# The first stage of a fused four-layer block: filler products at the start, small tables before tile 1, the turns of mem behind the third tile, index heads in two groups

## The reference

```python
h = x @ w_in                        # q_a, c_kv, q_idx, k_idx, w_idx, q_b, k_b, v_b, f_in
log_f = log_sigmoid(f_in + b_f);  cum_f = cumsum(log_f)
idx   = einsum('bthd,bsd->bths', q_idx, k_idx)          # 8 index heads of 64
score = einsum('bth,bths->bts', w_idx, relu(idx))       # causal, then top 64 keys
_, sel = top_k(score, 64)
# 8 heads of latent attention on the selected keys, with a bias by distance
# 8 heads of causal attention with cum_f[t] - cum_f[s] added to the logits
m = concat(o_a, o_b) @ w_o
mem_n = rmsnorm(mem, mem_norm_g)    # used from layer 2 on
```

## Time and profile before

| | us |
|---|---|
| median of three runs (1380.58 to 1381.6) | 1381.14 |
| the profiled execution | 1381.37 |
| its span, first to last instruction | 1380.1 |
| PE busy | 1346.4 |
| DVE busy | 1019.9 |
| ACT busy | 783.8 |
| POOL busy | 180.9 |

### The profile page before, as it was taken

The page is one execution under the profiler, slowest core; times in us unless marked ns, Lnnn a source line. Parts: engine busy times, 40 slices in busy tenths (PEclk is TensorE's granted clock), DMA queues, the critical chain, the costliest instruction groups (busy, mean ns, idle before and its releaser), DMA issues.

```text
span 1380.1 us, 20700 instructions
## 1 busy us (share of the span) xinstructions
PE 1346.4 (98%) x8171; PEld 1162.7 (84%) x8171; DVE 1019.9 (74%) x1684; ACT 783.8 (57%) x1260; POOL 180.9 (13%) x155
## 2 busy tenths in 40 slices
PE   7999999999999999999999999999999999899998
PEld 7886888888897888887977788888789998688887
DVE  5865588777887787777777577766567997777675
ACT  5654266555443666563667466555557785565553
POOL 4860300000200000000034200000302224000000
PEclk9999999999999999999999999999999999899999
DMA  8522255654563555553432165555344445355552
GB/s 317 222 85 116 99 206 213 231 195 175 195 234 123 213 214 214 185 197 136 185 123 93 44 231 213 214 184 194 141 171 165 147 143 194 123 189 199 188 195 76
DMA packets 37215, 240.85 MB, mean 175 GB/s; under 512 B 4096, under 2 KB 6528, under 8 KB 9728
## 3 DMA queue, kind: packets, MB, share of 16 engines
q1 hardware_dynamic: 37120, 239.54, 47.2%
HBM read 236.89 MB, written 2.64 MB: 174 GB/s over the span
## 4 chain that ended last, share of the span: by engine, by line
PE 88%; DVE 6%; ACT 2%; issue 2%; DMA 1%; POOL 1%; SPq 0%; DVEq 0%; ACTq 0%; POOLq 0%
PE ps L385 23%; PE ps L437 16%; PE ps L390 12%; PE ps L448 8%; PE ps L365 5%; PE ps L372 5%; PE ps L366 5%; PE ps L607 2%; PE ps L602 2%; PE ps L954 1%; DVE wlo L318 1%; PE ps L1865 1%; PE ps L580 1%; ACT whi L295 1%; PE ps L2173 1%
## 5 line engine op out<-in xcount | busy, mean ns | idle before, releaser
L318 DVE TENSOR_TENSOR wlo<-raw,whi 128x2048 fp32r<-128x2048 f32 (+1 forms) x178 | 398.7, 2246 | 106.6 <-ACT whi L295 104.5
L295 ACT ACTIVATE whi<-raw 128x2048 fp32r<-128x2048 f32 x203 | 385.8, 1904 | 83.0 <-PE ps L448 40.1
L385 PE MATMUL ps<-XS,whi 128*128 128x512 f32 x1408 | 338.4, 393 | 0.7 <-DVE XS L653 0.7
L385 PEld LDWEIGHTS ps<-XS,whi 128*128 128x128 f32 x1408 | 262.8, 189 | 54.6 <-issue 1.8
L437 PE MATMUL ps<-whi,MS 128*128 128x512 f32 x960 | 233.6, 391 | 0.0
L437 PEld LDWEIGHTS ps<-whi,MS 128*128 128x128 f32 x960 | 177.5, 188 | 35.9 <-issue 0.4
L303 POOL TENSOR_TENSOR wlo<-raw,whi 128x512 fp32r<-128x512 f32 x114 | 155.4, 1396 | 283.4 <-ACT whi L295 195.2
L390 PEld LDWEIGHTS ps<-XS,wlo 128*128 128x128 f32 x1408 | 180.5, 191 | 6.9
L390 PE MATMUL ps<-XS,wlo 128*128 128x256 f32 x1408 | 182.6, 283 | 0.0
L365 PE MATMUL ps<-XS,whi 128*128 128x256 f32 x672 | 166.9, 288 | 0.0
L366 PE MATMUL ps<-XS,whi 128*128 128x256 f32 x672 | 163.0, 283 | 0.0
(11 more groups left out here) (319 smaller groups left out, 1523.8 us busy)
## 6 DMA issues: line engine op xcount, KB each, us to landing
raw<-in_up SPq DMA_DIRECT2D x88, 1024.0 KB, 4.8
raw<-in_down SPq DMA_DIRECT2D x44, 1024.0 KB, 4.8
raw<-in_hg_t SPq DMA_DIRECT2D x16, 1024.0 KB, 4.8
raw<-in_od_t SPq DMA_DIRECT2D x8, 1024.0 KB, 5.2
raw<-in_ev_a SPq DMA_DIRECT2D x6, 1024.0 KB, 9.0
raw<-in_wa_o SPq DMA_DIRECT2D x6, 1024.0 KB, 4.9
raw<-in_hg_o SPq DMA_DIRECT2D x6, 1024.0 KB, 4.8
raw<-in_ev_o SPq DMA_DIRECT2D x4, 1024.0 KB, 5.8
```

What stands on the lines that cost most here:

```text
L295: ac.activation(parts_of(m)[0][:, 0:w], raw[m % NRAW][:, 0:w], ACT.Copy).then_inc(w_hi)
L318: ve.tensor_tensor(lo[:, c], r[:, c], hi[:, c].bitcast(F32), ALU.subtract).then_inc(w_lo_v)
L385: pe.matmul(banks[i][:, 0:512], hi[:, c], XS[:, k, 0:512], start=(k == 0), stop=False)
```

## The change

- Eight bf16 products of ones, 512 columns, stand ahead of the turns of x on PE. The ones are written by DVE into `gp`, which is unused then.
- One-hot table and `rel_bias` are loaded by one DMA each, in three copies, between tile 0 and tile 1 instead of behind it. The load of tile 3 is issued ahead of the mask and the large constants.
- On PE the turn of the gate rows (L1081) and tile 2 come ahead of `mem_pe`, and the index heads, formerly all between tiles 2 and 3, come as heads 0 to 3 behind tile 3 and 4 to 7 behind tile 4, each head by itself.
- On ACT the split of tile 4 and both copies of the index queries come ahead of `mem_act`, the split of tile 5 ahead of the heads; the log-sigmoid and the copies of tile 3 come between heads 3 and 4, the split of tile 6 behind head 7.
- On DVE the forget row comes between heads 3 and 4.

```diff
@@ -825,6 +825,7 @@
         rel, relp = ar[0:96, 9024:9032], ar[0:96, 9032:9036].bitcast(BF16)
         BIAS_BANK = [0, 1, 2, 3, 6, 7, 2, 3]
         r_pt = mark("r_pt")
+        idle = gp[:, 0:256].bitcast(BF16)
         x_bank = [[6, 7], [2, 3]]
 
         def bias_rows_pe(heads):
@@ -849,6 +850,9 @@
                 last.then_inc(m_tp.up())
 
         def prelude_pe():
+            pe.wait_ge(busy.sem, 1)
+            for _ in range(8):
+                pe.matmul(bank[0][:, :], idle[:, 0:128], idle, start=True, stop=True)
             pe.wait_ge(d_id, 16)
             for tt in range(2):
                 pe.wait_ge(d_x[tt], 16)
@@ prelude_dve
             ve.memset(mhalf, -0.5).then_inc(half.up())
+            ve.memset(idle, 1.0).then_inc(busy.up())
             for tt in range(2):
                 for q in range(2):
                     hi, lo, bv = x_views(tt, q)
@@ -903,7 +908,7 @@
         def prelude_pool():
             po.wait_ge(half.sem, 1)
 
-            po.wait_ge(d_oh, 96)
+            po.wait_ge(d_oh, 32)
             po.tensor_copy(relp, rel).then_inc(r_pt.up())
             po.wait_ge(r_pt.sem, 1)
             po.tensor_tensor(rel[32:64], rel[32:64], relp[32:64], ALU.subtract).then_inc(r_pt.up())
@@ -922,15 +927,17 @@
             sp.dma_start(cc[:, 0:128], T["c_f32"][:, 0:128]).then_inc(d_id, 16)
             for i in range(2):
                 sp.dma_start(xn[:, i, :], T["x"][0, 128 * i:128 * i + 128]).then_inc(d_x[i], 16)
+            sp_weights(0)
+            hot, par = T["c_onehot"], T["c_par"]
+            sp.dma_start(onehot, bass.AP(tensor=hot.tensor, offset=hot.offset, ap=[[0, 3], [384, 32], [1, 384]])).then_inc(d_oh, 16)
+            sp.dma_start(rel, bass.AP(tensor=par.tensor, offset=par.offset + PC["relb"][0],
+                                      ap=[[0, 3], [NPC, 32], [1, 8]])).then_inc(d_oh, 16)
             sp_weights(1)
             sp.dma_start(pc[:, :], T["c_par"]).then_inc(d_pc, 16)
-            a, b = PC["relb"]
-            for i in range(3):
-                sp.dma_start(onehot[32 * i:32 * i + 32], T["c_onehot"]).then_inc(d_oh, 16)
-                sp.dma_start(rel[32 * i:32 * i + 32], T["c_par"][0:32, a:b]).then_inc(d_oh, 16)
             sp_weights(2)
             for i in range(2):
                 sp.dma_start(gb[:, i, :], T["mem_2"][0, 128 * i:128 * i + 128]).then_inc(d_mem[i], 16)
+            sp_weights(3)
             sp.dma_start(mask, T["c_mask"]).then_inc(d_cb, 16)
             sp.dma_start(cc[:, 128:], T["c_f32"][:, 128:]).then_inc(d_cc, 16)
             sp_weights(4)
@@ -1072,31 +1079,18 @@
             bias_rows_pe(range(6))
             project(ea + 1, bank[5])
             bias_rows_pe((6, 7))
-            mem_pe()
             pe.wait_ge(b_out.sem, 6)
-            project(ea + 2, bank[6])
             pe.wait_ge(e_ac.sem, 1)
-            pe.wait_ge(x_lo.sem, 4)
             for tt in range(2):
                 ins = pe.transpose(bank[7][:, 16 * tt:16 * tt + 16], FW[0:16, 128 * tt:128 * tt + 128], ident[0:16, 0:16])
             ins.then_inc(e_fw.up())
-            for h in range(0, 8, 2):
-
-                pe.wait_ge(e_ac.sem, 3 + h // 4)
-                if h >= 4:
-                    pe.wait_ge(e_re.sem, h - 2)
-                else:
-                    pe.wait_ge(m_ev.sem, 8)
-                for tt in range(2):
-                    a, b = esegs[tt]
-                    c = 256 * (h // 2) + 128 * tt
-                    for r in range(2):
-                        q = slice(64 * r, 64 * r + 64)
-                        ins = pe.matmul(bank[(h + r) % 4][:, a:b], QI[q, c:c + 128], KI[q, 0:b - a], start=True, stop=True)
-                        if tt == 1:
-                            ins.then_inc(e_ix.up())
+            project(ea + 2, bank[6])
+            mem_pe()
+            pe.wait_ge(e_ac.sem, 2)
             project(ea + 3, bank[4])
+            index_heads(range(0, 4))
             project(ea + 4, bank[5])
+            index_heads(range(4, 8))
             project(ea + 5, bank[6])
             pe.wait_ge(e_wi.sem, 1)
             project(ea + 6, bank[7])
@@ -1140,6 +1134,22 @@
                     latent_query(i - 6)
             output(eo, 8, ms_ready(E0, lambda k: (k + 4) % 8))
 
+        def index_heads(heads):
+            for h in heads:
+                if h < 4:
+                    pe.wait_ge(e_ac.sem, 3)
+                    pe.wait_ge(m_ev.sem, 8)
+                else:
+                    pe.wait_ge(e_ac.sem, 4)
+                    pe.wait_ge(e_re.sem, h - 3)
+                r = h % 2
+                q = slice(64 * r, 64 * r + 64)
+                for tt in range(2):
+                    a, b = esegs[tt]
+                    c = 256 * (h // 2) + 128 * tt
+                    ins = pe.matmul(bank[h % 4][:, a:b], QI[q, c:c + 128], KI[q, 0:b - a], start=True, stop=True)
+                ins.then_inc(e_ix.up())
+
         def score_b(o, h):
             c = 256 * h
             pe.wait_ge(e_ac.sem, max(AT_QB[h // 2], AT_KB[h // 2]))
@@ -1210,6 +1220,13 @@
                 pe.matmul(ePAIR[p % 2][64 * r:64 * r + 64, 0:256], WV[:, 64 * (h + r):64 * (h + r) + 64], OA[r], start=True,
                           stop=True).then_inc(e_po.up())
 
+        def index_act(heads):
+            for h in heads:
+                ac.wait_ge(e_ix.sem, h + 1)
+                if h >= 2:
+                    ac.wait_ge(e_sc.sem, 2 * h - 2)
+                ac.activation(RR[h % 2], bank[h % 4][:, 0:384], ACT.Relu).then_inc(e_re.up())
+
         def even_act():
             def out_of(m, i, dst, scale=1.0):
                 ac.wait_ge(w_done, DONE[m])
@@ even_act: weights and QI
-                if j:
-                    mem_act()
                 ac.wait_ge(w_done, DONE[ea + 1 + j])
                 ac.activation(QI[:, 512 * j:512 * j + 512], bank[5 + j][:, :], ACT.Copy, scale=0.125).then_inc(e_ac.up())
-            for h in range(8):
-                ac.wait_ge(e_ix.sem, h + 1)
-                if h >= 2:
-                    ac.wait_ge(e_sc.sem, 2 * h - 2)
-                ac.activation(RR[h % 2], bank[h % 4][:, 0:384], ACT.Relu).then_inc(e_re.up())
+            mem_act()
             act_weights(ea + 5)
+            index_act(range(0, 4))
             z = slice(0, 104)
             ac.wait_ge(e_fz.sem, 1)
             ac.wait_ge(e_fw.sem, 1)
@@ -1256,6 +1268,7 @@
             out_of(ea + 3, 0, CT)
             ac.wait_ge(d_skw, 16)
             heads_of(ea + 3, 1, QX, 0, 0.125)
+            index_act(range(4, 8))
             for j in range(3):
                 act_weights(ea + 6 + j)
                 heads_of(ea + 4 + j, 0, KX, j)
@@ -1299,14 +1312,8 @@
 
         e_sc = mark("e_sc")
 
-        def even_dve():
-            ve.wait_ge(m_tp.sem, 4)
-            for r in range(2):
-                ve.memset(hx4(KX, r)[64 - 64 * r:128 - 64 * r], 0.0).then_inc(dv.up())
-            ve.wait_ge(e_fw.sem, 1)
-            ve.tensor_scalar(WI, bank[7][:, 0:32], float(np.float32(8 ** -0.5)), None, ALU.mult).then_inc(e_wi.up())
-            ve.wait_ge(e_wi.sem, 1)
-            for h in range(8):
+        def index_dve(heads):
+            for h in heads:
                 r = RR[h % 2]
                 ve.wait_ge(e_re.sem, h + 1)
                 for tt in range(2):
@@ -1317,6 +1324,27 @@
                     else:
                         ve.wait_ge(e_sc.sem, e_sc.n - 1)
                         ve.scalar_tensor_tensor(S[:, a:b], r[:, a:b], w, S[:, a:b], ALU.mult, ALU.add).then_inc(e_sc.up())
+
+        def even_dve():
+            ve.wait_ge(m_tp.sem, 4)
+            for r in range(2):
+                ve.memset(hx4(KX, r)[64 - 64 * r:128 - 64 * r], 0.0).then_inc(dv.up())
+            ve.wait_ge(e_fw.sem, 1)
+            ve.tensor_scalar(WI, bank[7][:, 0:32], float(np.float32(8 ** -0.5)), None, ALU.mult).then_inc(e_wi.up())
+            ve.wait_ge(e_wi.sem, 1)
+            index_dve(range(0, 4))
+            z = slice(0, 104)
+            ve.wait_ge(e_ac.sem, 1)
+            ve.tensor_scalar(FZ[z, :], FW[z, :], col("bf", 0, 104), None, ALU.add).then_inc(e_fz.up())
+            ve.wait_ge(e_ab.sem, 1)
+            ve.tensor_scalar(FZ[z, :], FZ[z, :], 0.0, None, ALU.min).then_inc(dv.up())
+            ve.wait_ge(dv.sem, dv.n)
+            ve.wait_ge(e_ln.sem, 1)
+            ve.tensor_tensor(FZ[z, :], FZ[z, :], FW[z, :], ALU.subtract).then_inc(dv.up())
+            ve.wait_ge(dv.sem, dv.n)
+            ve.wait_ge(d_cc, 16)
+            ve.tensor_tensor_scan(FW[z, :], C("ones", 104), FZ[z, :], 0.0, ALU.mult, ALU.add).then_inc(dv.up())
+            index_dve(range(4, 8))
             ve.wait_ge(d_cc, 16)
             ve.wait_ge(e_sc.sem, e_sc.n)
             ve.tensor_tensor(S[:, 0:128], S[:, 0:128], C("cmf"), ALU.add).then_inc(dv.up())
@@ even_dve, ahead of the memsets of QX: the forget row, L1336 to L1345, is gone from here
...
```

12 lines of the change are left out of this document (1 added, 11 removed).

## The result

The changed kernel takes 1398.73 us, the median of six runs from 1394.3 to 1403.6, beside 1381.37 for the kernel before on the same chip (six runs, 1376.7 to 1383.9): 1.0127 times as long, with an interval of [1.0109, 1.0145], 17.4 us more. I had forecast 1378.2 and a range to 1381.8; the time is far outside it and on the other side. The profiled execution took 1394.3 us (span 1393.0), the shortest of the six, 12.9 us above the one of before; what the profile explains is therefore these 12.9 us and not all of the 17.4. Two executions of the record, one of e11 at 4712.6 us and one of the kernel before at 1904.6, were in a slow state, far from all others, and count in no ratio.

What follows compares the result with a forecast made beforehand. PE, 98% busy, was taken as the bound, with savings only in its first 90 us: 3.0 + 0.5 + 1.0 + 2.7 = 7.2 us, cut by late DVE to 2.9; 1381.14 - 2.9 = 1378.2 us, range 1375.2 to 1381.8.

Steps and rivals of the forecast that it cites:

- turns of mem: PE's mem turns moved behind the third tile: 3.33 us become two bias rows and 16 unwaited turns, 1.0 us gained.
- a first relu after 40: Stated sign of a wrong forecast: head 0's relu on ACT before 37 or after 40; 38.5 was expected.
- POOL against DVE: DVE's L1363 beside POOL's run: left at its old 2.71 us, or waiting until POOL idles at 83.6, same sum.
- Four heads: ... 4.0 us: DVE's first four index heads, begun at 39.1, take 4.0 us, to 43.1.
- slower rival: Tile 5's load shares its queue with tile 6's and the store, landing about 41.4: 1384.0 us, chance 0.10.
- Products of ones: Filler on PE before x lands, to raise the clock: tile 0 ends 3.0 us earlier, bounds 0 and 3.5.
- Small tables: Six DMAs become two ahead of tile 1, delaying it 0.4 us; PE's wait for POOL's casts goes, 0.5 us.
- Heads in two groups: PE's index heads between tiles: cost 3.2 us instead of 5.96, 2.7 less; bounds of new cost 3.2 and 6.4.
- ACT splits tile 5 ahead of head 0: ACT splits tile 5 from 36.5 to 38.4 before head 0, so DVE begins the heads 2.9 us late.
- Tile 5 and 6 chain, POOL idle between them: Late split of tile 6 (50.6 to 52.5) makes POOL, with nothing between tiles 5 and 6, begin tile 6 at 52.6.
- One constant from 90 us on: From 90 us on, the profiles before and after should differ by one constant, a gain of 2.9 us.
- PE at tile 6: PE could take tile 6 at 50.3, waits 2.2 and 1.9 us for its parts, ends it at 60.2 instead of 63.5.

Runs made afterwards that it cites:

- e11: Changed kernel with POOL holding tile 3 until mem is scaled and tile 12 until the mask is written, tile 5's load before the bias table's store: 1380.7 us.
- e1: Changed kernel with POOL starting tile 3's low part only when DVE has scaled mem's rows: 1390.1 us, ratio 1.0068.
- e2: Changed kernel with tile 3's load back behind the mask and constants: 1393.4 us, ratio 1.0090.
- e7: Kernel before with only tile 3's load moved ahead of the mask and constants: 1386.5 us, ratio 1.0050.
- e4: Changed kernel without products of ones, with old table loads and tile 3's load at its old place; only the new engine orders stay: 1390.2 us, ratio 1.0068.
- e8: Changed kernel with only tile 5's load issued ahead of the bias table's store: 1392.1 us, ratio 1.0083.
- e10: e1 with a second POOL wait, tile 12's low part starting only when DVE has written the mask: 1384.8 us, ratio 1.0032.
- e16: e11 with a third POOL wait, tile 5's low part starting only when the first four heads are done: 1378.7 us, ratio 0.9988.
- e5: Kernel before with only the eight products of ones and their memset added: 1380.0 us, ratio 0.9993.
- e17: e10 with ACT's split of tile 5 moved behind the first four heads: 1380.0 us, ratio 0.9994.
- e15: e11 with a third POOL wait, tile 5's low part starting only behind DVE's first update of head 4: 1385.6 us, ratio 1.0041.
- e6: Kernel before with only both small tables loaded by two DMAs ahead of tile 1: 1383.1 us, ratio 1.0010.
- e9: e1 with tile 5's load issued ahead of the bias table's store: 1387.1 us, ratio 1.0043.

## Why the prediction was wrong

The step that failed is the sentence on the turns of mem: "DVE's root of the squares ... is done by 27.3, some 0.6 earlier than before". I kept the root's length (3.9 us, 21.64 to 25.52), though the same change loads tile 3 sooner and so puts POOL beside it. It was done at 36.1, and mem was scaled at 37.5. e1, e2 and e7 show this from both sides. The number itself was misread: before, the root was done at 25.52 and mem scaled at 26.98, and the 27.9 that I took off from is the end of the bias copies behind them. The test that I had named, a first relu after 40, came true at 50.81.

Next, "POOL against DVE". I had seen that L1363 took 2.71 us and left it there "at the old length", or waiting for a POOL run that ends at 83.6, "the sum is the same". Both halves failed: the run no longer ends with tile 11, because a late DVE lets tile 12 join it, and shut out to the end costs 7.65 us (e1, e2, e4, e8). In the profiled execution of the changed kernel the threshold itself got in at 1.48, and the mask group lost only 1.9. By e10 against e1 the term is worth 5 us, and I had it at nothing.

The Trainium skill ("GPSIMD Engine Reference", Key points) names this contention for two-port modes and two SBUF inputs. The traces agree that it is there, for operations on 128x2 too (1.14 to 1.25 and 6.55 us); in which mode those with one input ran, no run here shows. That sentence has no price and nothing on runs without gaps, and by it alone neither number could have been had.

A third term, "Four heads: ... 4.0 us", is part of what keeps even e11 (1380.7) above my 1378.2. I had seen POOL free only for the forget row and kept the heads at the old pace, but POOL has tile 5 beside them: they took 6.3 us in the changed kernel (51.39 to 57.64) and 6.6 in e11, whose first two instructions are

```profile
39.52 2.54 DVE L1327 TENSOR_SCALAR ar<-ar 128x128 f32<-128x128 f32 x2 [4.82 <-ACT ar L1232]
```

and 2.8 in e16 (38.77 to 41.59), with POOL held. The forget row behind them went the other way: 4.2 us in the changed kernel (57.64 to 61.88) against the 5.5 I took. That e16 lands at 1378.7, near my number, does not bear the forecast out: it has three waits and an early load that the forecast's kernel lacks.

The slower rival had the right gate and the wrong mechanism. Its threshold, a landing of tile 5 at 39.4 from which each microsecond is lost, gives 9.5 us for the landing at 48.9, the larger part of the 12.9 in the profiles. But the load was not late by sharing the queue: 10.0 us from issue against the 8.7 of the earlier trace rows are 1.3 of the 11.8 us by which it landed late. It was asked for 10.6 us late.

Point by point for the rest:

- *Products of ones*: right that they cost nothing, from 1.48 to 5.07, and the turns are quicker (2.62 us for 16, predicted 2.0, before 3.65). Tile 0's end was predicted 3.0 us earlier; it came 0.9 earlier in the changed kernel (17.07) and 2.4 in e5, and neither reached the end, since the casts or the loads are next. The products behind the pause of 2.08 us still were 0.22 apart, with a granted clock of 0.50 in 10 to 12 us, the 1.2 GHz level. The other traces with the filler do not go by the pause: the products were 0.13 apart behind 1.64 and 1.75 us (e5, e16) and also behind 2.16 and 3.02 (e10, e17), but at the lower level behind 1.87 and 2.51 (e15, e11), and in e7 they were 0.13 apart without any filler. The Trainium skill ("TensorE: Matmul & The Clock Gate", What you observe) has the point differ from run to run, and that agrees.
- *Small tables*: the order to PE was right (no wait before L836), the price wrong. I reckoned 0.4 us by their bytes. Tile 1 was split at 15.48 instead of 12.01, 3.5 later: SP issued its load 1.7 later (4.75 instead of 3.05, behind two more DMAs to issue), and it took 1.8 longer to land (10.7 instead of 8.9). DMA moved 254 GB/s in 10 to 12 us, and POOL's casts began at 13.19, not 10. e6 has the same in the old kernel (split at 16.06).
- *Heads in two groups*: right, 16 products in 1.68 us for four heads against the 1.6 taken; the lower bound of the disputed cost holds.
- *ACT splits tile 5 ahead of head 0*: right as a mechanism, and e11 against e10, e9 against e1 and e17 against e10 price it at 3 to 5 us; I had 2.9 late.
- *Tile 5 and 6 chain, POOL idle between them*: right, POOL had 9.89 us idle before tile 6.
- *One constant from 90 us on*: right to about 1.5 us (14.4 at 181 us, 12.9 at the end), with the wrong sign.
- *PE at tile 6*: 50.3 is right for a tile with three ahead of it, 40.42 + 3 x 5.76 - 7.2 = 50.5, but my bracket names two and a group of heads, which gives 46.3; nothing hangs on it.

What the profile of before had to offer: rows 21.64 to 25.36 of its root, 0.67 and 1.22 us for the two that met POOL and 0.16 for the ten that did not. I had read the group as one span. A factor of seven between instructions of one size was the warning.

## What to carry to other kernels

Where an instruction of one engine shows two lengths in a trace, find what the other engines did at both, and ask of each moved load whom it will start beside it: an earlier transfer started POOL's long stream beside DVE's critical little ones, and with what came late behind them 17 us were lost. A stream without gaps on POOL wants gaps placed by hand at DVE's critical places, a wait until the root, the heads or the mask is done; three such waits and one load moved were worth 20 us here, and one placed a step too late (e15) cost 7. A saving on an engine that is then late for another's work (the filler) is to be counted only behind that next wait.
